# Beginning the expert weights' transfers from two engines instead of one, in a two-block transformer kernel on one Trainium2 core

## The chip, the cores and the metric

One core of one Trainium2 chip. The metric is the device time of one launch in microseconds (us), the median of the runs shown. The kernel is one program with five instruction streams: TensorE (PE), VectorE (DVE), ScalarE (ACT), GpSimd (POOL) and SyncE (SP). The streams meet only at semaphores. A transfer (DMA) is begun by one of the streams and then moved by 16 DMA engines, which all streams share.

## What is computed

Two transformer blocks run one behind the other on 256 tokens of width 1024, all in float32. The first block has two mixers and a gated convolutional feed-forward part. The second has a pooling mixer, latent attention, and then the part that this change touches, a mixture of 32 experts of which each token uses 4:

```python
logits = ht @ w_router + b_router
top_vals, top_idx = top_k(logits, 4); gates = softmax(top_vals)
...
gu   = xblk @ w_gate_up[e] + b_gate_up[e]        # 1024 -> 2048
gate = minimum(gu[:, :1024], 7); up = clip(gu[:, 1024:], -7, 7)
act  = gate * sigmoid(1.702 * gate) * (up + 1)
yb   = act @ w_down[e] + b_down[e]               # 1024 -> 1024
y[token] += gate_of_token * yb
```

Every expert brings 8 MB of `w_gate_up` and 4 MB of `w_down`, whatever number of tokens it has. The 32 experts together are 12.58 MB x 32 = 402.7 MB.

## The kernel before

**Jobs.** A job is 64 token slots of one expert. An expert with more than 64 tokens has a second job, which uses the same weights again. PE runs the jobs in one loop (`job_turn`, L2246). A job is, in order: the gate and up product in four pairs of weight chunks (`gate_up`, L2112, its matmuls at L2127), with the combining matmuls of the job before after the second and third pair (L2162); the turn of the gate weights, the gathering of the next job's tokens, the turn of the activations and the next job's bias (L2149 to L2151, L2108, L2140, L1950); and the down product in two halves (`down`, L2190, its matmuls at L2203).

**Buffers.** An expert's weights stand in twelve slots, which are taken two by two as six places of 2 MB: pairs 0 to 3 for gate and up, and down halves 0 and 1. Three more places (`stage`, AHEAD = 3) hold pairs 0 to 2 of the expert behind it. So pairs 0 to 2 are loaded into `stage` and copied by GpSimd into their places (L599, four copies for a pair), while pair 3 and the down halves are loaded straight into theirs. A place is free when PE has used it: `gu_used` counts pairs 0 to 2, `gu_full` counts pair 3, `d_used` the quarters of the down product. For an expert with two jobs it is the second job that frees them (`last_job`, read from a table). For the last six experts (from STAGED = 26 on) there is no staging; pairs 0 to 2 too are loaded straight into their places when these are free.

**Who begins what.** Before the change SP begins every one of these transfers, 192 of 2 MB, in one order written out by hand, and it waits at each in turn. For one expert m of the main loop (L428 to L435):

```python
next_last_pair(m, last)      # wait gu_full of expert m,  begin pair 3 of m + 1
next_stage(m, 0)             # wait pair 0 of m + 1 copied, begin pair 0 of m + 2
for h in range(2):
    next_down(m, last, h)    # wait d_used of m, begin down half h of m + 1
next_stage(m, 1)
next_stage(m, 2)
```

In the six experts without staging (L440 to L447) the order is pairs 0, 1, 2, 3 and the halves 0, 1. In the table of issues, L373 is a pair into its place, L376 a pair into `stage`, L379 a down half and L444 a pair of the unstaged experts.

**GpSimd's stream** (`gpsimd_program`, L462) does small work for the first block and attention, among it two subtractions for the output projection (L585, PE reads their results at L2041), the reciprocal roots (`rsqrt`, L483), and then the loop of copies (L591 to L600): for each of the pairs 0 to 2 it waits until the staged pair has landed and until PE has used that pair's place, and copies.

**The start.** Expert 0's six places and expert 1's staged pairs are loaded during attention, as buffers come free; `jobs_ready` (the order of the jobs) then opens the loops. The places lie partly over the attention's buffers, so each of these loads has a wait of its own (L382 to L399).

Of the kernel before, what the change touches and what calls it, by code (L numbers as in the profile page):

```python
# [32 lines left out]
P = 128  # L33
# [237 lines left out]

def slot_use(n):

    return n % RING, 16 * (n // RING + 1)
# [32 lines left out]
def sync_program(g, sp):  # L307
# [61 lines left out]
    gate_up = w["w_gate_up_2"].rearrange("e (c p i) n -> e c p (i n)", p=P, i=2)  # L369
    down = w["w_down_2"].rearrange("e (h p i) n -> e h p (i n)", h=2, p=P)  # L370
# [6 lines left out]

    def load_down(e, h):
        sp.dma_start(pair_slot(g, PAIRS + h), down[e, h]).then_inc(s.job_landed(GU + 2 * h), 16)  # L379
# [8 lines left out]
    load_gu(0, 3)  # L388
    load_down(0, 1)
# [7 lines left out]
    load_down(0, 0)  # L397
# [12 lines left out]
    def next_last_pair(m, last):  # L410

        sp.wait_ge(s.gu_full, last * 2 + 2)
        load_gu(m + 1, PAIRS - 1)

    def next_down(m, last, h):

        sp.wait_ge(s.d_used, last * DN + (2 * h + 2))
        load_down(m + 1, h)

    sp.wait_ge(s.jobs_ready, 1)  # L420
    last = last_job(0)
    next_stage(0, 0)
    next_stage(0, 1)
    next_last_pair(0, last)
    next_stage(0, 2)
    for h in range(2):
        next_down(0, last, h)
    with sp.Fori(1, STAGED - 2) as m:  # L428
        last = last_job(m)
        next_last_pair(m, last)  # L430
        next_stage(m, 0)
        for h in range(2):
            next_down(m, last, h)
        next_stage(m, 1)
        next_stage(m, 2)  # L435
    last = last_job(STAGED - 2)
    next_last_pair(STAGED - 2, last)
    for h in range(2):
        next_down(STAGED - 2, last, h)
    with sp.Fori(STAGED - 1, E - 1) as m:  # L440
# [4 lines left out]
        next_last_pair(m, last)  # L445
        for h in range(2):
            next_down(m, last, h)  # L447
# [14 lines left out]
def gpsimd_program(g, pool):  # L462
# [117 lines left out]
    pool.tensor_tensor(t.diff[:], t.diff[:], t.u_pad[:, :, 16:], ALU.subtract).then_inc(s.diff_ready, 1)  # L580
    rsqrt("pool")
    for c in range(2):
# [5 lines left out]
    rsqrt("moe")  # L588

    pool.wait_ge(s.jobs_ready, 1)  # L590
    with pool.Fori(0, STAGED - 1) as m:  # L591
        last = pool.value_load(t.job_last[0:1, bass.ds(m, 1)], min_val=0, max_val=E + OVER - 1)
        for pair in range(AHEAD):
# [6 lines left out]
            ins.then_inc(s.in_place[pair], 16)  # L600

# [978 lines left out]
def tensor_program(g, pe):  # L1580
# [531 lines left out]
    def gate_up(m, o, e, pair):  # L2112
# [3 lines left out]
        if m is None or pair == PAIRS - 1:  # L2116
            pe.wait_ge(*expert_landed(g, e, 2 * pair))
        else:
            pe.wait_ge(s.in_place[pair], e * 16 + 16)
# [70 lines left out]
    def down(m, o, e):  # L2190
# [454 lines left out]
```

## Time and profile before

| what | value |
|---|---|
| time, median of 3 runs | 1493.42 us (1492.33 to 1495.0) |
| the profiled execution: span from first to last instruction | 1490.6 us |
| median less the profiled span | 2.8 us |
| mean granted TensorE clock | 0.989 of full speed |
| bytes read from HBM | 479.26 MB, 322 GB/s over the span |
| first transfer of an expert's weights begun | 484.17 us |
| order of the jobs known, loop of copies starts | 548.19 us |
| last byte of the weights lands | shortly after 1470 us |

No time beside its span is given for the profiled execution itself, so its own time is taken as the span and the 2.8 us that the median has over it; the lowest run is 1.7 us over the span.

How to read it: the page gives the busy time of each engine and cuts the span into 40 slices of 37.3 us, with the busy tenths of each engine and of the DMA engines and the GB/s moved. The chain of waits follows the work that ended last back to what released it. A timeline lists an engine's instructions in order of time, with the idle time before one and what ended it. The windows give the busy time of each engine and the DMA share in chosen stretches.

### The profile page before, as it was taken

To read this page: it belongs to the slowest core of one execution; us is meant where nothing else is said; L and a number is where in the kernel's file an instruction comes from. 1 tells how busy PE (TensorE), PEld (TensorE's weight loads), DVE (VectorE), ACT (ScalarE), POOL (GpSimd) and SP (SyncE) were. 2 spreads that over 40 slices of the span, in tenths; PEclk is the share of its full clock that TensorE was granted. 3 is DMA by queue.
4 is the path that set the end of the run, shared out by engine and by line. 5 is a ranking of instruction groups with operands and counts; after the bars stand their busy time and mean duration, and the time that the engine had idled before them with its cause. 6 is when DMAs were issued, how large, how long until landed. Compare 5 with 4: busy or idle time off the path is not lost.

```text
span 1490.6 us, 20373 instructions
## 1 busy us (share of the span) xinstructions
PE 1415.9 (95%) x7344; PEld 781.2 (52%) x7345; DVE 650.3 (44%) x1102; ACT 248.9 (17%) x424; POOL 416.3 (28%) x432
## 2 busy tenths in 40 slices
PE   8999999999989999999999999999999999999995
PEld 7668867999976664343333343343333334333332
DVE  3134735677654553344443344444444434333333
ACT  1222113444423420010001010010000001000001
POOL 3000011222216233334433435444443444200000
PEclk9999999999999999999999999999999999999998
DMA  8433344455533878999996999999999999999995
GB/s 276 147 136 113 113 134 149 170 196 174 177 126 135 300 283 358 429 427 427 429 427 276 429 429 427 427 427 428 429 427 427 427 428 429 427 427 429 427 429 226
DMA packets 77413, 480.73 MB, mean 323 GB/s; under 512 B 7019, under 2 KB 31272, under 8 KB 52808
## 3 DMA queue, kind: packets, MB, share of 16 engines
q1 hardware_dynamic: 74046, 477.45, 78.6%
q10 hardware_dynamic: 3338, 2.88, 0.6%
q8 instruction: 20, 0.33, 0.1%
q14 instruction: 9, 0.07, 0.0%
HBM read 479.26 MB, written 1.05 MB: 322 GB/s over the span
## 4 chain that ended last, share of the span: by engine, by line
PE 51%; DMA 39%; POOL 5%; DVE 3%; issue 1%; ACT 1%; SPq 0%; POOLq 0%; ACTq 0%; DVEq 0%
DMA stage<-in_w_gate_up 28%; PE bank L2127 10%; PE bank L1866 8%; PE bank L1614 8%; DMA ring<-in_w_gate_up 7%; PE bank L1624 6%; PE bank L2203 5%; POOL ring L599 5%; PE bank L1878 4%; PE bank L1798 2%; DMA ring_b<-in_w_gate_up 2%; DMA ring_b<-in_w_down 2%; PE bank L2108 1%; PE bank L1675 1%; PE bank L2162 1%
## 5 line engine op out<-in xcount | busy, mean ns | idle before, releaser
L599 POOL COPY ring<-stage 128x1024 f32<-128x1024 f32 x300 | 310.3, 1080 | 443.7 <-DMA stage<-in_w_gate_up 359.7
L2127 PE MATMUL bank<-ring,x_T 128*64 128x512 f32 x1584 | 368.0, 610 | 38.1 <-POOL ring L599 31.3
L2127 PEld LDWEIGHTS bank<-ring,x_T 128*64 128x64 f32 x1584 | 111.0, 140 | 272.6 <-issue 205.9
L2203 PE MATMUL bank<-ring_b,act_T 128*64 128x512 f32 x1056 | 236.1, 596 | 1.1 <-ACT act_T L872 0.5
L1494 DVE TENSOR_TENSOR h<-h,bank 128x512 f32<-128x512 f32 x128 | 82.2, 683 | 243.9 <-PE bank L2162 243.9
L2203 PEld LDWEIGHTS bank<-ring_b,act_T 128*64 128x64 f32 x1056 | 72.0, 137 | 147.9 <-issue 125.7
L2127 PE MATMUL bank<-ring_b,x_T 128*64 128x512 f32 x528 | 120.6, 598 | 2.3 <-DMA ring_b<-in_w_gate_up 2.3
L1470 DVE SCALAR_TENSOR_TENSOR y_lo<-bank,slot_gate,y_hi 128x512 fp32r<-128x512 f32 x33 | 24.8, 751 | 194.8 <-ACT y_hi L852 194.8
L866 ACT ACTIVATE sig<-bias_raw 128x512 f32<-128x512 f32 x33 | 20.8, 629 | 509.5 <-DVE bias_raw L1500 509.5
L1866 PE MATMUL bank<-h_hi,ff_hi 128*128 128x256 f32 x352 | 99.8, 284 | 1.9 <-POOL h_lo L531 1.4
L1866 PE MATMUL bank<-h_lo,ff_hi 128*128 128x256 f32 x352 | 99.6, 283 | 0.0
L1866 PE MATMUL bank<-h_hi,ff_lo 128*128 128x256 f32 x352 | 99.6, 283 | 0.0
L1614 PE MATMUL bank<-x_nT,ring 128*128 128x256 f32 x448 | 98.1, 380 | 0.0
L524 POOL TENSOR_TENSOR ff_lo<-ring,ff_hi 128x2048 fp32r<-128x2048 f32 x11 | 51.0, 4640 | 159.0 <-PE bank L1866 111.1
L1614 PEld LDWEIGHTS bank<-x_nT,ring 128*128 128x128 f32 x448 | 84.7, 190 | 12.2 <-issue 0.8
L2127 PEld LDWEIGHTS bank<-ring_b,x_T 128*64 128x64 f32 x528 | 35.0, 136 | 71.3 <-issue 67.2
L1866 PEld LDWEIGHTS bank<-h_hi,ff_hi 128*128 128x128 f32 x352 | 67.5, 192 | 2.8 <-issue 1.7
L2108 PE MATMUL bank<-picks,h_half 128*128 128x128 f32 x512 | 68.1, 286 | 0.0
L738 ACT ACTIVATE ff_hi<-ring 128x2048 fp32r<-128x2048 f32 x33 | 61.8, 1903 | 35.6 <-DMA ring<-in_w_ffn_in 35.6
L1866 PEld LDWEIGHTS bank<-h_lo,ff_hi 128*128 128x128 f32 x352 | 67.5, 192 | 0.4
L1866 PEld LDWEIGHTS bank<-h_hi,ff_lo 128*128 128x128 f32 x352 | 67.5, 192 | 0.0
L2108 PEld LDWEIGHTS bank<-picks,h_half 128*128 128x128 f32 x512 | 62.8, 196 | 0.8 <-issue 0.8
(435 smaller groups left out, 1609.4 us busy)
## 6 DMA issues: line engine op xcount, KB each, us to landing
stage<-in_w_gate_up SPq DMA_DIRECT2D x75, 2048.0 KB, 25.0
ring_b<-in_w_down SPq DMA_DIRECT2D x64, 2048.0 KB, 23.0
ring_b<-in_w_gate_up SPq DMA_DIRECT2D x32, 2048.0 KB, 20.9
ring<-in_w_gate_up SPq DMA_DIRECT2D x21, 2048.0 KB, 25.5
ring<-in_w_in SPq DMA_DIRECT2D x22, 1024.0 KB, 7.2
ring<-in_w_ffn_in SPq DMA_DIRECT2D x22, 1024.0 KB, 5.1
ring<-in_w_ffn_out SPq DMA_DIRECT2D x11, 1024.0 KB, 4.7
ring<-in_w_out SPq DMA_DIRECT2D x8, 1024.0 KB, 6.1
```

The source lines that it names most:

```text
L524: pool.tensor_tensor(t.ff_lo[:, 1, :], t.ring[:, slot, :], t.ff_hi[:, slot, :].bitcast(F32), ALU.subtract).then_inc(s.ff_lo_pool, 1)
L599: ins = pool.tensor_copy(pair_slot(g, pair)[:, cols], t.stage[:, pair, cols])
L738: act.activation(t.ff_hi[:, n % RING, :], t.ring[:, n % RING, :], ACT.Copy).then_inc(s.ff_hi_done, 1)
L1494: dve.tensor_tensor(t.h[:, b, cols], t.h[:, b, cols], g.banks[2 + c][:], ALU.add).then_inc(s.added, 1)
L1614: ins = pe.matmul(bank[:, j * T:(j + 1) * T], wk[:, f * P:(f + 1) * P], src[:, k, :], start=(k == 0), stop=(k == len(weights) - 1))
L1624: ins = pe.matmul(bank[:, 0:n], src[:, k, b * P:(b + 1) * P], wk[:, c0:c0 + n], start=(k == 0), stop=(k == len(weights) - 1))
L1798: ins = pe.matmul(bank[:, q * T:(q + 1) * T], chunk(g, n, (4, 512))[:, k, P * (f % 4):P * (f % 4) + P], (t.o_sb, t.o_glaT)[q][:, k, :], st ...
L1866: ins = pe.matmul(bank[:, f * T:(f + 1) * T], wt[:, k, f * P:(f + 1) * P], ht[:, k, :], start=(k == 0 and part == 0), stop=(k == KT - 1 an ...
L1878: ins = pe.matmul(banks[2 * b + c][:], ut[:, q, k, b * P:(b + 1) * P], wt[:, k, 512 * c:512 * c + 512], start=False, stop=last, skip_group ...
L2108: ins = pe.matmul(banks[6][:, f * P:(f + 1) * P], t.h_half[:, b, k_rows], t.picks[:, b, :], start=(b == 0), stop=(b == 1))
L2127: ins = pe.matmul(banks[n][rows, :], t.x_T[:, c, :], job_slot(g, c)[:, c0:c0 + 512], start=False, stop=(c == GU - 1), skip_group_check=True)
L2203: ins = pe.matmul(banks[4][rows, :], t.act_T[:, k, SLOTS * (c // 2):SLOTS * (c // 2) + SLOTS], job_slot(g, GU + c)[:, c0:c0 + 512], start= ...
```

## The change

SP keeps only what it loads into `stage` (and pairs 0 to 2 of the unstaged experts). GpSimd begins pair 3 and both down halves of every expert, behind its copies for the same expert. Pair 3 and the halves count on semaphores of their own.

```diff
@@ SP, start
     sp.dma_start(t.b_down[0:E, :], w["b_down_2"]).then_inc(s.b_down_in, 16)
-    load_gu(0, 3)
-    load_down(0, 1)
...
     load_gu(0, 2)
-    load_down(0, 0)
     for pair in range(1, AHEAD):
         load_stage(1, pair)
@@ SP, loops
+    for pair in range(AHEAD):
+        next_stage(0, pair)
+    with sp.Fori(1, STAGED - 2) as m:
+        for pair in range(AHEAD):
+            next_stage(m, pair)
     sp.wait_ge(s.jobs_ready, 1)
-    last = last_job(0)
-    next_stage(0, 0)
-    next_stage(0, 1)
-    next_last_pair(0, last)
-    next_stage(0, 2)
-    for h in range(2):
-        next_down(0, last, h)
-    with sp.Fori(1, STAGED - 2) as m:
-        last = last_job(m)
-        next_last_pair(m, last)
-        next_stage(m, 0)
-        for h in range(2):
-            next_down(m, last, h)
-        next_stage(m, 1)
-        next_stage(m, 2)
-    last = last_job(STAGED - 2)
-    next_last_pair(STAGED - 2, last)
-    for h in range(2):
-        next_down(STAGED - 2, last, h)
     with sp.Fori(STAGED - 1, E - 1) as m:
         last = last_job(m)
         for pair in range(AHEAD):
             sp.wait_ge(s.gu_used, last * AHEAD + (pair + 1))
             sp.dma_start(pair_slot(g, pair), gate_up[m + 1, pair]).then_inc(s.in_place[pair], 16)
-        next_last_pair(m, last)
-        for h in range(2):
-            next_down(m, last, h)
@@ GpSimd
+    def load_last_pair(e):
+        pool.dma_start(pair_slot(g, PAIRS - 1), gate_up[e, PAIRS - 1]).then_inc(s.pair_landed, 16)
+    def load_down(e, h):
+        pool.dma_start(pair_slot(g, PAIRS + h), down[e, h]).then_inc(s.half_landed[h], 16)
+    def next_straight(m, last):
+        pool.wait_ge(s.gu_full, last * 2 + 2)
+        load_last_pair(m + 1)
+        for h in range(2):
+            pool.wait_ge(s.d_used, last * DN + (2 * h + 2))
+            load_down(m + 1, h)
+
     rsqrt("pool")
+    pool.wait_ge(*g.r2.drained("s7"))
+    load_last_pair(0)
+    load_down(0, 1)
     for c in range(2):
...
     rsqrt("mla")
     rsqrt("moe")
+    pool.wait_ge(*g.r2.filled("pa11"))
+    load_down(0, 0)
 
     pool.wait_ge(s.jobs_ready, 1)
     with pool.Fori(0, STAGED - 1) as m:
...
             ins.then_inc(s.in_place[pair], 16)
+        next_straight(m, last)
+    with pool.Fori(STAGED - 1, E - 1) as m:
+        next_straight(m, last_job(m))
@@ PE
-        if m is None or pair == PAIRS - 1:
+        if pair == PAIRS - 1:
+            pe.wait_ge(s.pair_landed, e * 16 + 16)
+        elif m is None:
             pe.wait_ge(*expert_landed(g, e, 2 * pair))
...
-                pe.wait_ge(*expert_landed(g, e, GU + c))
+                pe.wait_ge(s.half_landed[c // 2], e * 16 + 16)
```

## Rows read from the trace of the kernel before

**Rows 1.** The page: busy tenths and GB/s of the DMA engines in 40 slices.

```profile
DMA  8433344455533878999996999999999999999995
GB/s 276 147 136 113 113 134 149 170 196 174 177 126 135 300 283 358 429 427 427 429 427 276 429 429 427 427 427 428 429 427 427 427 428 429 427 427 429 427 429 226
```

**Rows 2.** Chain of waits, a combining, and one steady turn: start us, us, what.

```profile
828.68 0.67 PE bank L2162 x4
...
985.83 25.03 DMA stage<-in_w_gate_up
1011.09 4.00 POOL ring L599 x4
```

**Rows 3.** Windows over the steady stretch; columns PE, PEld, DVE, ACT, POOL, PEclk, DMA share, GB/s.

```profile
1000.00:1100.00 100.00, 93.53 (x465) 36.63 (x465) 40.44 (x70) 8.61 (x21) 39.93 (x38) 0.98 1.01 428
```

**Rows 4.** Timeline of PE, job start without a stall (650 us) and with stalls (1009 us).

```profile
624.50 7.04 PE L2127 MATMUL bank<-ring,x_T 128*64 128x512 f32 x32
...
650.71 7.04 PE L2127 MATMUL bank<-ring,x_T 128*64 128x512 f32 x32
...
1009.48 3.60 PE L2127 MATMUL bank<-ring,x_T 128*64 128x512 f32 x16
1015.13 3.65 PE L2127 MATMUL bank<-ring,x_T 128*64 128x512 f32 x16 [2.05 <-POOL ring L599]
```

**Rows 5.** Timeline of SP's queue, steady stretch: the fourth pair and a staged pair.

```profile
998.74 0.34 SPq L373 DMA_DIRECT2D ring_b<-in_w_gate_up  x1
1001.55 0.33 SPq L376 DMA_DIRECT2D stage<-in_w_gate_up  x1
```

**Rows 6.** Timeline of GpSimd, the steady stretch: the copy of pair 0.

```profile
996.39 4.98 POOL L599 COPY ring<-stage 128x1024 f32<-128x1024 f32 x4 [5.82 <-DMA stage<-in_w_gate_up]
```

**Rows 7.** Windows at the loops' start and the first DMA gap, columns as in rows 3.

```profile
552.00:556.00 4.00, 3.93 (x21) 1.32 (x19) 3.79 (x6) 0.45 (x2) 4.00 (x5) 1.00 0.73 213
...
584.00:588.00 4.00, 4.00 (x23) 1.48 (x21) 2.57 (x4) 0.63 (x1) 3.74 (x4) 1.00 0.17 74
588.00:592.00 4.00, 4.00 (x31) 3.23 (x33) 1.73 (x4) 1.10 (x4) 0.00 (x0) 1.00 0.81 262
```

**Rows 8.** Timelines there: GpSimd's copies of three pairs, then SP's next issues.

```profile
575.87 11.88 POOL L599 COPY ring<-stage 128x1024 f32<-128x1024 f32 x12 [15.27 <-PE bank L2127]
...
587.82 0.35 SPq L373 DMA_DIRECT2D ring_b<-in_w_gate_up  x1
588.45 0.34 SPq L376 DMA_DIRECT2D stage<-in_w_gate_up  x1
```

**Rows 9.** Windows at the second gap, columns as in rows 3.

```profile
792.00:796.00 4.00, 4.00 (x22) 1.38 (x20) 2.09 (x9) 0.10 (x1) 1.03 (x2) 1.00 0.88 373
...
804.00:808.00 4.00, 4.00 (x26) 2.05 (x23) 2.60 (x4) 1.07 (x3) 2.85 (x3) 1.00 0.09 20
```

**Rows 10.** Timelines there: the second job of expert 8 (PE), copies, SP's issue behind it.

```profile
791.19 7.04 PE L2127 MATMUL bank<-ring,x_T 128*64 128x512 f32 x32
...
794.97 11.87 POOL L599 COPY ring<-stage 128x1024 f32<-128x1024 f32 x12 [22.70 <-PE bank L2127]
...
806.93 0.34 SPq L373 DMA_DIRECT2D ring_b<-in_w_gate_up  x1
```

**Rows 11.** The end: PE's last fourth pair and last down product, and the DMA window.

```profile
1462.77 3.65 PE L2127 MATMUL bank<-ring_b,x_T 128*64 128x512 f32 x16 [0.58 <-DMA ring_b<-in_w_gate_up]
...
1469.64 7.09 PE L2203 MATMUL bank<-ring_b,act_T 128*64 128x512 f32 x32 [0.47 <-ACT act_T L872]
...
1468.00:1472.00 4.00, 3.11 (x16) 1.47 (x18) 0.36 (x1) 0.66 (x2) 0.00 (x0) 1.00 0.65 274
```

**Rows 12.** Attention: GpSimd's two subtractions and PE's first use of their results.

```profile
499.08 9.02 POOL L585 TENSOR_TENSOR ring_r<-ring,pa_hi 128x2048 fp32r<-128x2048 f32 x2 [4.62 <-ACT pa_hi L827]
...
515.84 0.40 PE L2041 MATMUL bank<-ring_r,ya_hi 128*128 128x512 f32 x1
```

**Rows 13.** Window in which only transfers with 2 KB rows (w_in) are in flight.

```profile
20.00:25.00 5.00, 5.00 (x25) 4.41 (x24) 0.00 (x0) 1.11 (x2) 0.00 (x0) 1.00 1.11 357
```

More of the change, by code:

```diff
@@ L269, in _, with expert_weights @@
             tensor_program(g, pe)
+def expert_weights(w):
+    return (w["w_gate_up_2"].rearrange("e (c p i) n -> e c p (i n)", p=P, i=2),
+            w["w_down_2"].rearrange("e (h p i) n -> e h p (i n)", h=2, p=P))
 def slot_use(n):
@@ L365, in sync_program @@
         load(g.n_second + n, src, shape)
-    gate_up = w["w_gate_up_2"].rearrange("e (c p i) n -> e c p (i n)", p=P, i=2)
-    down = w["w_down_2"].rearrange("e (h p i) n -> e h p (i n)", h=2, p=P)
+    gate_up, _ = expert_weights(w)
     def load_gu(e, pair):
@@ L376, in load_stage @@
         sp.dma_start(t.stage[:, pair, :], gate_up[e, pair]).then_inc(s.staged[pair], 16)
-    def load_down(e, h):
-        sp.dma_start(pair_slot(g, PAIRS + h), down[e, h]).then_inc(s.job_landed(GU + 2 * h), 16)
     sp.wait_ge(*g.r2.filled("pm1"))
@@ L408, in next_stage @@
         load_stage(m + 2, pair)
[L410 to L418, printed above, removed]
-    sp.wait_ge(s.jobs_ready, 1)
-    last = last_job(0)
-    next_stage(0, 0)
-    next_stage(0, 1)
-    next_last_pair(0, last)
-    next_stage(0, 2)
-    for h in range(2):
-        next_down(0, last, h)
-    with sp.Fori(1, STAGED - 2) as m:
-        last = last_job(m)
-        next_last_pair(m, last)
-        next_stage(m, 0)
-        for h in range(2):
-            next_down(m, last, h)
-        next_stage(m, 1)
-        next_stage(m, 2)
-    last = last_job(STAGED - 2)
-    next_last_pair(STAGED - 2, last)
-    for h in range(2):
-        next_down(STAGED - 2, last, h)
+    for pair in range(AHEAD):
[3 more added lines that the diff above has]
+            next_stage(m, pair)
+    sp.wait_ge(s.jobs_ready, 1)
     with sp.Fori(STAGED - 1, E - 1) as m:
@@ L580, in gpsimd_program, with last_job @@
     pool.tensor_tensor(t.diff[:], t.diff[:], t.u_pad[:, :, 16:], ALU.subtract).then_inc(s.diff_ready, 1)
+    gate_up, down = expert_weights(g.w)
+    def load_last_pair(e):
+        pool.dma_start(pair_slot(g, PAIRS - 1), gate_up[e, PAIRS - 1]).then_inc(s.pair_landed, 16)
+    def load_down(e, h):
+        pool.dma_start(pair_slot(g, PAIRS + h), down[e, h]).then_inc(s.half_landed[h], 16)
+    def last_job(e):
+        return pool.value_load(t.job_last[0:1, bass.ds(e, 1)], min_val=0, max_val=E + OVER - 1)
+    def next_straight(m, last):
[4 more added lines that the diff above has]
+            load_down(m + 1, h)
     rsqrt("pool")
+    pool.wait_ge(*g.r2.drained("s7"))
+    load_last_pair(0)
+    load_down(0, 1)
     for c in range(2):
@@ L588, in gpsimd_program @@
     rsqrt("moe")
+    pool.wait_ge(*g.r2.filled("pa11"))
+    load_down(0, 0)
     pool.wait_ge(s.jobs_ready, 1)
     with pool.Fori(0, STAGED - 1) as m:
-        last = pool.value_load(t.job_last[0:1, bass.ds(m, 1)], min_val=0, max_val=E + OVER - 1)
+        last = last_job(m)
         for pair in range(AHEAD):
@@ L2399, in __init__ @@
         self.place_free = new("place_free")
+        self.pair_landed = new("pair_landed")
+        self.half_landed = [new(f"half_landed{h}") for h in range(2)]
         self.in_place = [new(f"in_place{n}") for n in range(AHEAD)]
```

## The prediction

> **What bounds the kernel now.** I read the slices first: from the seventeenth on the DMA engines are busy nine tenths or more and move 427 to 429 GB/s, except in the slice at 783 us (276 GB/s) and in the last [rows 1]. The window over 100 us of that stretch says the same: DMA share 1.01, 428 GB/s [rows 3]. So from about 590 us the kernel is bound by bytes. One expert is 12.58 MB, at 428 GB/s 29.4 us, or 4.9 us for each of its six transfers. The chain of waits shows how this looks from inside: a staged transfer takes 25.03 us, its copy 4.00 us, and with some 0.2 us between them the turn is 29.4 us [rows 2]. The 25 us are no latency to be saved; they are five transfers of 4.9 us that stand ahead in the one queue. PE alone needs less: a job without a stall starts 26.21 us after the one before it (624.50 to 650.71) [rows 4]. So PE is idle 3.2 us per expert, and the DMA engines are not.
>
> Two gaps in the DMA's work are all that an order of issue can win. The first is at 584 to 592 us (shares 0.17 and 0.81, so 3.3 + 0.8 = 4.1 us idle) [rows 7]. GpSimd has copied three pairs by 587.75, the first of them by 579.9, but SP stands at the fourth pair's wait until 587.82 and begins the staged pair behind it at 588.45 [rows 8]. The second is the only place where an expert has two jobs. The DMA engines run dry at about 795.5 us (share 0.88 of a window of 4 us) and are idle until about 807.6 (0.09) [rows 9]. The second job starts at 791.19, the copies at 794.97, the first copy is done at 799.0, and SP again comes to it only behind the fourth pair at 806.93 [rows 10].
>
> **The change part by part.**
>
> *SP loses 96 of its 192 issues and all waits for PE in the staged stretch.* SP's own time is no bound (0.33 us an issue) [rows 5]. What goes is the block: a staged pair is begun as soon as it is copied. At the first gap that is 579.9 instead of 588.45, so the DMA engines stay busy: 4.1 us won. At the second it is 799.0 instead of 806.93: 7.9 us won, if PE stands where it stood.
>
> *GpSimd gets 96 issues.* No row shows an issue by GpSimd. The nearest are SP's 0.33 us [rows 5] and, on GpSimd itself, one copy, 4.98/4 = 1.2 us at its longest [rows 6]; I take 1.2 us. Three of them are 3.7 us per expert, beside 12 to 13 us of copies in a period of 29.4 us: hidden by GpSimd's idle time (5.82 us ahead of that copy alone). If this cover were gone, the copy of pair 0 would be late, and it has slack: it ends at 1001.4, PE needs it at 1009.48 [rows 4, 6]. In attention two issues come ahead of the subtractions, into the 4.62 us in which GpSimd idles, and their results are first read at 515.84, 7.7 us after they end [rows 12]. At nothing, then; if an issue cost 4 us or more, PE would begin to wait there.
>
> The copy of 4.98 us, where the undisturbed one takes 4.00 [rows 2, 6], shows that GpSimd can be held up by about 1 us in a pair. The Trainium skill (SBUF — State Buffer, Who interferes with whom) says that VectorE in a two-port mode locks GpSimd out, and that a transfer begun by GpSimd then waits for its descriptors. It speaks against this change; by it a begin would be late by the length of a VectorE instruction, which the sum doesn't need while the other queue has work.
>
> *Order behind the copies.* GpSimd begins pair 3 of expert m+1 behind the copy of its pair 2, where SP needed only `gu_full` of m. Behind the waiting GpSimd stand both down halves and the next copies. In before's steady stretch pair 3 is begun at 998.74 [rows 5], while the copy of pair 1 starts only at 1011.09 [rows 2]: the old order of landings would not survive. What settles in its place I work out next.
>
> *Two queues instead of one.* This is the term that decides. In one queue the bytes arrive in the order in which PE uses them. In two, with three transfers of an expert each, I assume equal shares: each then gets 9.8 us per transfer while both have work. Bounds: GpSimd's queue served first is nearly the old order; SP's served first ends as below, since SP can be ahead by its three staged places only. When the down half 1 of expert e lands, SP's queue has then moved as many transfers as GpSimd's: all of the staged pairs of e+1 and 0.9 of the first of e+2. Before, it was only the first of e+1. So 2.9 transfers, 14 us of bytes, come ahead of what PE waits for. PE waits for down halves instead of staged pairs, and stands later behind the same bytes. The rate itself stays: with both queues never empty the period is still 29.4 us.
>
> Put into numbers at the second gap: GpSimd's 21 transfers for experts 1 to 7 and SP's 21.9 are 42.9 x 4.902 = 210.3 us. From the loops' first byte at 553.1 (share 0.73 of the window from 552) [rows 7] that is 763.4, and 1.8 us between last byte and landing (worked out at the end, below) make 765.2. Half a down product later (7.09/2 = 3.55) [rows 11] expert 8 starts, at 768.8, and its second job 26.2 later at 795.0, 3.8 after the 791.19 of before. The DMA engines drain early, but they restart by PE: before, the first copy was done 7.8 us after the job's start (799.0), so now at 802.8, against SP's 806.93. **Won: 4.1 us**; of the 4.1 and 7.9 together, two thirds are given back. Behind it the bytes run without a gap, as before.
>
> *The end.* Before, the last byte arrives at about 1470.6 (share 0.65 of a 4 us window); the wait for the fourth pair ended at 1462.77, and the down product ends at 1476.73 [rows 11], 13.96 us later. In the new order the last SP transfer (pair 2 of expert 31) lands while GpSimd's queue still has 1.3 to 1.55 transfers, 6.3 to 7.6 us; I take 7.0. With a last byte at 1470.6 - 4.1 = 1466.5 that is 1459.5, and 1.8 us from byte to landing (before: 1470.6 - 9.8 = 1460.8, landed 1462.6) make 1461.3. PE then does pair 2 (3.6) [rows 4] and a combining (0.67) [rows 2] ahead of the same tail: 1461.3 + 0.15 + 3.6 + 0.67 = 1465.7, + 13.96 = 1479.7 against 1476.73. **Lost: 7.1 us at the end, 3.0 net of the 4.1 won.**
>
> The 1.3 to 1.55 are found so: PE has used pair 2 of expert 30 at a time S, which begins pair 2 of 31; SP's queue, always full, lands it 29.4 - 3.6 = 25.8 later. Down half 1 of expert 30 lands 9.0 to 11.6 after S (pair 3, turns, gathering and a half product lie between), and in the 14.2 to 16.8 us that are left GpSimd's queue moves 1.45 to 1.7 of its last three.
>
> Sum: 1490.6 + 3.0 = 1493.6 us of span; with the 2.8 us that the median has over the span, 1496.4, which is 3.0 over the median 1493.42.
>
> **The rivals.** A measurement of this kernel can tell about 0.2% (3 us) from no change; that bounds "same".
>
> *A, forecast: bytes bound, PE pushed back by the equal shares.* 1493.5 to 1502: the loss of 7.1 may be 4 to 10 and the 4.1 won 1.5 to 4.1 (issues of 1.2 us and small gaps make PE later still). For it: the full DMA share. Against: the equal share is an assumption. Chance 0.42, a third of it under 1496.4.
>
> *B, faster: GpSimd's queue is served promptly, PE keeps its place.* Then both gaps close: 4.1 + 7.9 = 12.0 us, 1481.4; with half of that, 1487. Decided by whether the down halves land as early against the staged pairs as before. For it: the gaps are real and SP's block is what holds them. It takes an uneven share, or GpSimd's queue being mostly the shorter. Chance 0.22.
>
> *C, no change: the gain at the second gap is larger or the last pair less late, and they cancel.* 1490.4 to 1496.4; 1493.4 if 3 us of the tail's loss fall away. Chance 0.18.
>
> *D, clearly slower: transfers begun by GpSimd move less per us.* Nothing in the trace has one. If they moved as those with 2 KB rows did, 357 instead of 428 GB/s [rows 13], half the 402.7 MB would take 564 instead of 470 us: +94. The other way no slice moves over 429 [rows 1], which is 2 us less for all of it. I take none, since both queues move the same 16 KB rows; 2% on that half is +9, 5% is +24. It decides from about 1% on. Chance 0.18, mostly 1502 to 1525.
>
> The Trainium skill (DMA: Bandwidth & Descriptors, Queues, rings and completion order) has each DMA engine take turns between queues packet by packet; with rows of equal length that gives the equal shares of A. The same page (Issuing engines are not separate DMA queues) says that beginning on several engines saves only issue time, by which nothing but C is left.
>
> Range: A and C whole, of B the nearer half, of D the nearer part: 1485 to 1512. The likeliest case alone: 1493.5 to 1502. Faster by over 0.2%: B and a little of C, 0.25. Within: the rest of C and a third of A, 0.29. Slower: two thirds of A, and D, 0.46.
>
> **What would show it.** In the chain of waits the staged transfer should give way to down halves, pair 3 and unstaged pairs; PE should wait 2 to 3 us per expert at the down product (L2203); staged pairs should land well before their copy. The share at 584 to 592 should be 1.0; the second gap should start earlier than 795.5 and end near 803. DMA share and 428 GB/s elsewhere should stay, and PE's last fourth pair should start later relative to the last byte. Wrong would be: a rate below 420 or above 432 GB/s, gaps in each period (GpSimd's order starves the DMA), or a second job that starts no later than 791.

## The result and the profile after

| | kernel before | changed kernel |
|---|---|---|
| median | 1495.76 us (1492.33 to 1498.94, 6 runs) | 1505.65 us (1501.65 to 1507.97, 6 runs) |
| ratio, 95% interval | | 1.0065 [1.0047, 1.0083] |

The change makes the kernel slower by 0.65%. The forecast had the side (slower) and the range (1485 to 1512), but not the size: +3.0 us against +9.9 (a second comparison, below, gives +9.9 again). The measured time lies above the likeliest case alone (1493.5 to 1502); only the width that was added for rival D reaches it. The profiled execution spans 1505.2 us.

In the changed kernel the gate and up product stands at L2131, the down product at L2207, GpSimd's copies at L598, its begins of pair 3 at L557 and of the down halves at L561, and SP's staged pairs at L381. The page of the changed kernel (slices, queues, chain, groups with busy time, mean ns and idle time before, issues with us to landing):

```profile
DMA  8433343555525679999995999999999999999993
GB/s 274 157 123 112 112 160 125 189 176 188 184 91 178 252 301 427 428 428 426 429 428 215 430 427 428 428 426 429 427 428 428 426 429 428 392 429 428 429 427 132
...
q1 hardware_dynamic: 60222, 276.11, 46.4%
q0 software_dynamic: 13824, 201.33, 31.5%
...
DMA ring_b<-in_w_down 31%; PE bank L2207 10%; PE bank L2131 10%; PE bank L1868 8%; PE bank L1616 7%; DMA ring<-in_w_gate_up 7%; PE bank L1626 6%; PE bank L1880 4%; PE bank L1800 2%; PE bank L2110 1%; PE bank L1677 1%; PE bank L2166 1%; PE bank L2025 1%; PE bank L1952 0%; PE bank L2097 0%
...
L2207 PE MATMUL bank<-ring_b,act_T 128*64 128x512 f32 x1056 | 249.0, 620 | 40.6 <-DMA ring_b<-in_w_down 40.1
...
L561 POOL DMA_DIRECT2D ring_b<-in_w_down x64 | 33.9, 529 | 297.8 <-PE bank L2207 297.8
...
stage<-in_w_gate_up SPq DMA_DIRECT2D x75, 2048.0 KB, 21.0
ring_b<-in_w_down POOLq DMA_DIRECT2D x64, 2048.0 KB, 21.6
ring_b<-in_w_gate_up POOLq DMA_DIRECT2D x32, 2048.0 KB, 15.6
```

The rate is what it was, 426 to 430 GB/s [rows 1]. The slice of the second gap (at 783 us before, at 790 us now) has gone from 276 to 215 GB/s, and there is a new dip, 392 GB/s, in the slice that begins at 1279 us, where staging ends. PE now waits at the down product for down halves: 40.1 us over the loops. The chain confirms the turn foretold: 25 us of a down half, then half a down product, where a staged transfer and its copy stood [rows 2]. That half product takes 3.7 us, or 5.4 us where the granted clock fell from 2.4 to 1.2 GHz behind the wait (0.57 of full speed in the window 1084:1088; PE had been busy 1.35 of the 4 us before). The chain around 1060 us:

```profile
1058.51 25.05 DMA ring_b<-in_w_down
1083.56 0.04 issue
1083.61 5.38 PE bank L2207 x16
```

The DMA view of the same kernel's window 1000:1100 (queue: packets, MB, share of 16 engines) and its line in the windows answer to [rows 3]:

```profile
q1 hardware_dynamic: 1469, 21.45, 50.5%
q0 software_dynamic: 1461, 21.32, 50.1%
```

```profile
1000.00:1100.00 100.00, 93.25 (x458) 35.62 (x454) 32.17 (x74) 7.95 (x19) 51.07 (x54) 0.98 1.01 428
```

Here the two queues, which both have work, share the engines equally, to 1%, at the old rate of 428 GB/s. So rival D (GpSimd's transfers are slower) is out, and A's assumption of equal shares holds.

The first gap is closed: the windows 584:588 and 588:592 have shares of 1.02 and 1.00, where there were 0.17 and 0.81 [rows 7]. The second gap in the changed kernel, in windows:

```profile
792.00:796.00 4.00, 4.00 (x29) 3.01 (x31) 1.61 (x3) 1.10 (x4) 0.00 (x0) 1.00 0.29 123
...
808.00:812.00 4.00, 4.00 (x22) 1.31 (x20) 1.28 (x2) 0.00 (x0) 4.00 (x5) 1.00 0.35 70
...
1280.00:1284.00 4.00, 3.92 (x28) 2.83 (x28) 2.38 (x5) 1.06 (x4) 4.00 (x4) 1.00 0.61 258
1284.00:1288.00 4.00, 4.00 (x20) 1.29 (x18) 1.07 (x3) 0.00 (x0) 0.65 (x2) 1.00 0.77 246
```

These places have to be counted from the start of the loops: GpSimd's began 3.6 us later in this execution, at 551.8 instead of 548.19 us. Ahead of that PE's granted clock was 0.83 of full speed in 508:512, 0.50 (1.2 GHz) in 512:520 and 0.89 in 520:524, after PE had been busy 3.03 of the 4 us in 504:508; the repeat below, with 3.15 there, had 1.00 throughout, and its loops began at 547.86. The account is made on the repeat.

### The profile page after: what moved, and what is told of

Read it like the earlier page. It is cut to its first block, busy times and chain, and to the rows that moved or that the text cites. A ratio compares the mean times of both kernels' runs of the same rounds, so it can differ in the third digit from the quotient of the medians.

```text
span 1505.2 us, 20326 instructions
## 1 busy us (share of the span) xinstructions
PE 1422.4 (94%) x7344; PEld 788.3 (52%) x7345; DVE 601.2 (40%) x1102; ACT 248.9 (17%) x424; POOL 473.0 (31%) x528
## 4 chain that ended last, share of the span: by engine, by line
PE 56%; DMA 37%; DVE 3%; issue 1%; ACT 1%; POOL 0%; POOLq 0%; SPq 0%; DVEq 0%; ACTq 0%
DMA ring_b<-in_w_down 31%; PE bank L2207 10%; PE bank L2131 10%; PE bank L1868 8%; PE bank L1616 7%; DMA ring<-in_w_gate_up 7%; PE bank L1626 6%; PE bank L1880 4%; PE bank L1800 2%; PE bank L2110 1%; PE bank L1677 1%; PE bank L2166 1%; PE bank L2025 1%; PE bank L1952 0%; PE bank L2097 0%
## 5 line engine op out<-in xcount | busy, mean ns | idle before, releaser
L598 POOL COPY ring<-stage 128x1024 f32<-128x1024 f32 x300 | 316.1, 1106 | 157.8 <-PE bank L2131 84.6
L2131 PE MATMUL bank<-ring,x_T 128*64 128x512 f32 x1584 | 356.7, 599 | 8.0 <-DMA ring<-in_w_gate_up 7.6
L2207 PE MATMUL bank<-ring_b,act_T 128*64 128x512 f32 x1056 | 249.0, 620 | 40.6 <-DMA ring_b<-in_w_down 40.1
L2131 PEld LDWEIGHTS bank<-ring,x_T 128*64 128x64 f32 x1584 | 111.1, 138 | 229.8 <-issue 219.6
L2207 PEld LDWEIGHTS bank<-ring_b,act_T 128*64 128x64 f32 x1056 | 73.7, 142 | 198.6 <-issue 128.6
L561 POOL DMA_DIRECT2D ring_b<-in_w_down x64 | 33.9, 529 | 297.8 <-PE bank L2207 297.8
L2131 PE MATMUL bank<-ring_b,x_T 128*64 128x512 f32 x528 | 120.6, 598 | 0.0
L2131 PEld LDWEIGHTS bank<-ring_b,x_T 128*64 128x64 f32 x528 | 35.0, 136 | 68.7 <-issue 68.6
L854 ACT ACTIVATE y_hi<-bank,slot_gate 128x512 fp32r<-128x512 f32 x33 | 22.7, 687 | 287.1 <-PE bank L2207 287.1
```

The source lines that it names most:

```text
L561: pool.dma_start(pair_slot(g, PAIRS + h), down[e, h]).then_inc(s.half_landed[h], 16)
L598: ins = pool.tensor_copy(pair_slot(g, pair)[:, cols], t.stage[:, pair, cols])
L2131: ins = pe.matmul(banks[n][rows, :], t.x_T[:, c, :], job_slot(g, c)[:, c0:c0 + 512], start=False, stop=(c == GU - 1), skip_group_check=True)
L2207: ins = pe.matmul(banks[4][rows, :], t.act_T[:, k, SLOTS * (c // 2):SLOTS * (c // 2) + SLOTS], job_slot(g, GU + c)[:, c0:c0 + 512], start= ...
```

## The experiments

Each was timed beside the kernel before (medians of before 1493.05, 1493.0 and 1493.51 us in the three groups, 20 to 23 runs each). In the order in which they ran.

### 1. The changed kernel again

> The changed kernel once more, unaltered, as the yardstick for the runs beside it. Theory 1 (equal shares of two queues put staged pairs ahead of what PE waits for, so PE is pushed back; GpSimd's transfers themselves are as fast): about 1505 us, gap at the expert with two jobs from 793 to 810 us, last staged landing well ahead. In its first profile the loops of experts started 3.6 us later than before (551.8 against 548.2 us), beside a granted TensorE clock of half speed from 512 to 520 us. If the change causes that, the loops start near 551.8 again and the clock falls at the same place; if it is chance, it may start near 548 and the run is about 4 us shorter.

Measured: 1502.94 us (1501.32 to 1506.71), ratio 1.0072 [1.0055, 1.0089]; profiled span 1499.7 us. The timelines around expert 8's second job (PE, GpSimd, SP), two windows, PE's end, and SP's last store:

```profile
796.25 7.04 PE L2131 MATMUL bank<-ring,x_T 128*64 128x512 f32 x32
...
800.04 11.85 POOL L598 COPY ring<-stage 128x1024 f32<-128x1024 f32 x12 [28.65 <-PE bank L2131]
...
804.21 8.17 SPq L381 DMA_DIRECT2D stage<-in_w_gate_up  x3
```

```profile
788.00:792.00 4.00, 4.00 (x25) 1.80 (x25) 1.65 (x4) 0.66 (x2) 0.00 (x0) 1.00 0.27 115
...
804.00:808.00 4.00, 4.00 (x20) 1.24 (x20) 1.28 (x2) 0.00 (x0) 4.00 (x6) 1.00 0.72 217
...
1276.00:1280.00 4.00, 4.00 (x21) 1.45 (x22) 1.69 (x4) 0.66 (x2) 2.13 (x3) 1.00 0.45 131
...
1468.00:1472.00 4.00, 4.00 (x20) 1.21 (x18) 1.89 (x3) 0.00 (x0) 0.00 (x0) 1.00 0.67 279
```

```profile
1465.17 3.65 PE L2131 MATMUL bank<-ring,x_T 128*64 128x512 f32 x16 [1.23 <-DMA ring<-in_w_gate_up]
1469.41 3.65 PE L2131 MATMUL bank<-ring_b,x_T 128*64 128x512 f32 x16
...
1476.28 7.09 PE L2207 MATMUL bank<-ring_b,act_T 128*64 128x512 f32 x32 [0.47 <-ACT act_T L874]
...
1492.88 0.35 SPq L422 DMA_DIRECT2D out<-h  x1
```

The second job starts at 796.25 instead of 791.19 (+5.1); the first staged pair behind it is begun at 804.21, where SP's first begin was at 806.93 [rows 10]. The last byte comes at 1468 + 0.67 x 4 = 1470.7, as before (1470.6), but the down product ends at 1483.37, 12.7 us behind it, where it was 6.1 [rows 11].

This execution (1501.32 us) is the fastest of its six, and in it PE stands earlier than in the others. Counted from the start of the loops, in us (a version is the experiment of that number, here and below):

| profiled execution | second job of expert 8 | SP's first begin behind the gap | last byte | down product's end behind it | program's end behind that |
|---|---|---|---|---|---|
| before | 243.0 | 258.7 | 922.4 | 6.1 | 13.9 |
| version 2 (below) | 248.2 | 256.1 | 919.6 | 6.6 | 13.8 |
| version 1 | 248.4 | 256.3 | 922.8 | 12.7 | 16.3 |
| changed kernel, first profile | 250.3 | 258.2 | 925.0 | 12.1 | 16.3 |
| version 5 | 250.8 | 258.8 | 925.2 | 13.2 | 16.3 |
| version 7, first | 251.6 | 259.6 | 926.4 | 13.1 | 16.3 |
| version 8 | 250.2 | 258.2 | 925.1 | 7.8 | 14.0 |

So the restart behind the gap, 2.4 us earlier than before in version 1, is between 0.6 us earlier and 0.9 us later in the four other executions with two queues, and the last byte is 2.6 to 4.0 us later instead of 0.4. What decides between the two is not shown. The two columns at the end hardly move between executions of one kind.

### 2. The order alone, with one queue

```diff
@@ before, SP
     with sp.Fori(1, STAGED - 2) as m:
         last = last_job(m)
+        for pair in range(AHEAD):
+            next_stage(m, pair)
         next_last_pair(m, last)
-        next_stage(m, 0)
         for h in range(2):
             next_down(m, last, h)
-        next_stage(m, 1)
-        next_stage(m, 2)
```

(and likewise for expert 0, ahead of the loop).

> The kernel before with one queue only, SP beginning all, but in the order that the changed kernel has: staged pairs 0, 1, 2 of expert m+2, then pair 3 and the down halves of m+1. Theory 1: the bytes that come ahead of a down half are two transfers more than before (9.8 us), where two queues make it 2.9 to 3.4. Against the kernel before the second job starts about 3 us later (794), the DMA engines restart 4 to 5 us earlier (802 to 803), the first gap is closed and the end of the kernel is as before, since the unstaged experts keep their order: 1490 to 1494 us where before has 1495.8. Theory 2 (transfers begun by GpSimd are slow): there are none here, so at or below the kernel before. Theory 3 (pair 3 and the halves begun behind the copies starve the DMA or PE): as slow as the changed kernel, 1502 to 1506, with gaps in each period.

Measured: 1490.81 us (1488.03 to 1492.79), ratio 0.9986 [0.9977, 0.9996]; profiled span 1488.0. Its second job starts at 796.19 us, its first staged pair is begun at 804.15: both within 0.1 us of version 1's. So the order alone pushes PE by 5.2 us, with no second queue. But it does so by another wait. PE's waits for transfers between 600 and 790 us (in all, times, longest), in version 1 and in this version:

```profile
PE bank L2207 <- DMA ring_b<-in_w_down: 9.5, 5, 2.8
```

```profile
PE bank L2126 <- DMA ring_b<-in_w_gate_up: 10.0, 5, 3.1
```

Here PE waits for pair 3, ahead of which all three staged pairs now stand; in version 1 it waits for down halves. The agreement to 0.1 us is at least in part chance: in four of the five traces of two queues in the table the push is 7.2 to 8.6 us. In this version the push costs nothing: the last six experts are in the old order, PE has caught up by the end (down product ends at 1474.18), and the last byte comes at about 1467.6, 3.0 us earlier than before. Of the changed kernel's +9.9 us, then, the order of the staged stretch is -2.2, and the rest, +12.1, is what the second queue adds. By the two profiled executions (1499.7 less 1488.0 = 11.7) these are 3.1 of a later last byte, 6.1 of a later end behind it (12.7 against 6.6) and 2.5 behind the down product (16.3 against 13.8).

### 3. One staged pair ahead of pair 3, with one queue

```diff
@@ before, SP
     with sp.Fori(1, STAGED - 2) as m:
         last = last_job(m)
-        next_last_pair(m, last)
         next_stage(m, 0)
+        next_last_pair(m, last)
```

> The kernel before with one line moved: SP begins the staged pair 0 of expert m+2 ahead of pair 3 of m+1 (no other order changed, one queue). Theory 1: the first gap closes (4.1 us), at the second gap one transfer of 4.9 us fits into the 7.9 us, PE's lag hardly grows: 1487 to 1491 us where before has 1495.8. Theory 3: pair 3 is begun 2.8 us later in each steady period, PE waits for it and the gain is lost: 1494 to 1498.

Measured: 1488.72 us (1487.01 to 1490.73), ratio 0.9972 [0.9959, 0.9985]: faster than both kernels. The first gap is closed here too (window 584:588 at 1.07), and the second job is not pushed: it starts at 786.87. SP begins staged pair 0 at 794.82, as soon as it is copied. This is much of the gain that the change was after, for one line moved.

### 4. Pair 3 begun by GpSimd ahead of its copy of pair 2

```diff
@@ changed, GpSimd, loop of copies
         for pair in range(AHEAD):
             pool.wait_ge(s.staged[pair], m * 16 + 16)
             pool.wait_ge(s.gu_used, last * AHEAD + (pair + 1))
+            if pair == AHEAD - 1:
+                next_last_pair(m, last)
...
-        next_straight(m, last)
+        next_halves(m, last)
```

> The changed kernel with GpSimd beginning pair 3 of expert m+1 ahead of its copy of pair 2 instead of behind it. Theory 1: no change against the changed kernel (within 2 us, about 1505), since its queue is never empty when pair 3 is begun. Theory 3: half or more of the 10 us come back, 1495 to 1500. Theory 2: no change.

Measured: 1574.35 us (1573.09 to 1575.99), ratio 1.0545 [1.0528, 1.0563], which no theory had. VectorE's group in the window 1000:1100, the window, and PE's and GpSimd's timelines:

```profile
L1517 DVE SCALAR_TENSOR_TENSOR act<-bias_raw 128x512 f32<-128x512 f32 x4 | 18.0, 4497 | 0.1
```

```profile
1000.00:1100.00 100.00, 87.91 (x414) 34.89 (x416) 42.65 (x68) 7.92 (x20) 42.60 (x48) 0.93 0.98 407
```

```profile
998.24 4.50 DVE L1517 SCALAR_TENSOR_TENSOR act<-bias_raw 128x512 f32<-128x512 f32 x1
...
998.21 3.98 POOL L603 COPY ring<-stage 128x1024 f32<-128x1024 f32 x4
...
1002.79 0.75 PE L2151 MATMUL bank<-ident,act 128*128 128x128 f32 x4 [3.10 <-DVE act L1517]
```

The copy of pair 2 now begins when PE has finished the gate and up product (gu_full), at the moment at which VectorE works on the SwiGLU. Its last operation, both of whose inputs lie in SBUF, takes 4.50 us instead of 0.69, as long as the copy; PE waits 3.10 us for it in each job of this stretch, and the rate falls to 407 GB/s.

### 5. The same, with the copy kept off VectorE's operation

```diff
@@ version 4, GpSimd, behind next_last_pair
+                pool.wait_ge(s.act_ready, last + 1)
```

> The version that took 1574 us (the changed kernel with pair 3 begun ahead of the copy of pair 2), and in it GpSimd now waits, ahead of the copy of pair 2, until VectorE's SwiGLU for that job is done. Theory G (the 79 us came from GpSimd's copy running beside VectorE's operation with two inputs in SBUF, which then took 4.5 us instead of 0.7 and kept PE waiting 3.1 us per job): that operation is back at 0.7 to 0.8 us, PE no longer waits 3 us for act, period 29.4 us, and the time falls to 1497 to 1506 us. Rival (the time came from pair 3 standing ahead in GpSimd's queue, that is from the order of the bytes): it stays above 1550. Between: 1510 to 1530 if the later copy of pair 2 itself becomes the new wait.

Measured: 1504.65 us (1502.69 to 1511.41), ratio 1.0088 [1.0066, 1.0111]. The group is back, and so is the rate (428 GB/s):

```profile
L1518 DVE SCALAR_TENSOR_TENSOR act<-bias_raw 128x512 f32<-128x512 f32 x4 | 2.8, 692 | 0.1
```

One wait gives back 70 us, with pair 3 still early in the queue: the collision was the cause. And pair 3 early or late in GpSimd's queue makes no difference that was measured (1504.65 against 1502.94, ranges overlapping).

### 6. One GpSimd transfer, and 32

The kernel before, with the load of the down biases moved to GpSimd, as one transfer:

```diff
-    sp.dma_start(t.b_down[0:E, :], w["b_down_2"]).then_inc(s.b_down_in, 16)
...
+    pool.wait_ge(*g.r2.drained("s7"))
+    pool.dma_start(t.b_down[0:E, :], g.w["b_down_2"]).then_inc(s.b_down_in, 16)
```

> The kernel before, with one single transfer changed hands: GpSimd instead of SP begins the load of the down biases (128 KB, at the start). Disputed: the 2.4 us by which the changed kernel's program goes on longer behind its last down product (16.3 us against 13.9 us) although its output stores begin and move alike. Theory F (a fixed cost at program end as soon as GpSimd has a queue of its own): the span behind the last down product grows from 13.9 to about 16.3 us, and the median by 2 to 3 us over the kernel before, ratio 1.0015 to 1.002. Rival (it comes from many transfers outstanding on that queue, or from a PE clock or a landing by chance): 13.9 us as before, ratio 1.000.

Measured: 1493.89 us, ratio 1.0009 [0.9999, 1.0018]; the profiled execution ends 4.4 us after SP's last store is begun (1486.64, span 1491.0), as before (1486.21, 1490.6). The fixed cost is not there. With 32 transfers of one row:

```diff
+    for e in range(E):
+        pool.dma_start(t.b_down[e:e + 1, :], g.w["b_down_2"][e:e + 1, :]).then_inc(s.b_down_in, 16)
```

> The kernel before, and the down biases (128 KB) are loaded by GpSimd in 32 transfers of one row instead of one of SP. One GpSimd transfer had left the program's end at 4.4 us behind VectorE's last instruction; the changed kernel with 96 has 6.85 us. Theory N (the end grows with the number of transfers that GpSimd has begun): 5.2 us with 32 of them, +0.8. Rival P (it grows with the packets or bytes of that queue, or with transfers begun inside a loop): 4.4 us, unchanged. Their issues take some 17 us of GpSimd at 470 to 490 us; if that delays the subtractions for the output projection, the start moves by up to 5 us, which is read off separately.

Measured: 1492.76 us, ratio 0.9993 [0.9983, 1.0003], and again 4.4 us (1492.34, 1496.7). The number of begins is not it either.

### 7. Staging kept up to the last experts

`STAGED = E - 2` instead of `E - 6` in the changed kernel:

> The changed kernel with staging kept up for experts up to 30 (STAGED = E - 2) instead of 26. The changed kernel shows a DMA gap of 2.3 to 3.2 us where staging ends, because SP's queue has run dry there while GpSimd's has only its share; before has none. Theory T (the gap comes from SP waiting for PE to free a place of the first unstaged expert, which it now reaches early): the gap moves from 1280 us to about 1400 us and stays about as long, and the last pairs stay late, so that the time is within 2 us of the changed kernel's, 1502 to 1506. Rival (the six unstaged experts are what makes the tail late, since SP there is no longer ahead): the wait for the last SP transfer moves by several us; the time falls by 3 to 7 us, to 1496 to 1500.

Measured: 1505.72 us (1502.37 to 1508.02), ratio 1.0083 [1.007, 1.0096]. The dip has moved along, to the window 1396:1400 (share 0.46, so 2.2 us), as foretold. PE no longer waits for any SP transfer at the end, yet its down product still ends 13.1 us behind the last byte (1487.7 against 1474.6):

```profile
1453.73 7.09 PE L2207 MATMUL bank<-ring_b,act_T 128*64 128x512 f32 x32
...
1480.60 7.09 PE L2207 MATMUL bank<-ring_b,act_T 128*64 128x512 f32 x32 [0.47 <-ACT act_T L874]
```

PE's last wait for any transfer ends at 1375.22, for a down half of expert 27. From there it works without waiting for a transfer and still comes 13 us behind the last byte. So the end is set here by PE's own late place, with no late transfer; in version 1 the wait for the last SP transfer (1.23 us) comes on top.

`STAGED = E - 1` in version 3 (one queue):

> One queue, staged pair 0 begun ahead of pair 3 (the version at 1488.7 us, under both kernels), with staging kept up for all experts but the last (STAGED = E - 1). Theory: the end is set by the last bytes and what PE must still do behind them; with one queue there is no gap where staging ends, so it is within 1.5 us of 1488.7. Rival: staging the last experts too lets their pairs 0 to 2 land earlier than PE frees their places, the DMA engines are kept fuller at the end, and 2 to 5 us are won: 1484 to 1487.

Measured: 1489.67 us, ratio 0.998 [0.9971, 0.9989]: as the theory had it, no gain.

### 8. The last six experts with one queue

```diff
@@ changed, GpSimd
     with pool.Fori(STAGED - 1, E - 1) as m:
-        next_straight(m, last_job(m))
+        last = last_job(m)
+        for pair in range(AHEAD):
+            pool.wait_ge(s.gu_used, last * AHEAD + (pair + 1))
+            pool.dma_start(pair_slot(g, pair), gate_up[m + 1, pair]).then_inc(s.tail_in[pair], 16)
+        next_straight(m, last)
@@ changed, SP, in place of its loop over the unstaged experts
+    with sp.Fori(1, E - STAGED + 1) as m:
+        for pair in range(AHEAD):
+            sp.wait_ge(s.tail_in[pair], m * 16)
+            sp.sem_inc(s.in_place[pair], 16)
```

> The changed kernel, and in the last six experts (those without staging) GpSimd begins all six transfers in the order of the kernel before, pairs 0, 1, 2, 3 and the halves; SP begins none there and only passes their landing on. So one queue instead of two from 1280 us on, everything ahead of it as changed. Theory (the loss at the end is the equal share of two queues, by which the last SP transfer lands 5.5 us before the last byte and not 9.8): the wait for the last pair 2 at L2131 goes away, the last wait is again that for pair 3, the down product ends 13 to 14 us behind it as before, and 5 to 7 us are won: 1496 to 1498 us. The 2.4 us at the very end stay. Rival (PE is late at the end because of its pushed place, whatever the queues): 1501 to 1504, as the changed kernel.

Measured: 1497.89 us (1493.81 to 1501.07), ratio 1.0024 [1.0012, 1.0035]; profiled span 1496.4. PE's end and SP's last store:

```profile
1466.79 3.65 PE L2134 MATMUL bank<-ring_b,x_T 128*64 128x512 f32 x16 [0.54 <-DMA ring_b<-in_w_gate_up]
...
1491.94 0.35 SPq L421 DMA_DIRECT2D out<-h  x1
```

The last wait is again that for pair 3, 7.9 us before the last byte (1466.79 and 1474.7; in before 1462.77 and 1470.6, so 7.8). Over its own before it stands at +4.4 us where version 1 stands at +9.9: 5.5 us won, as the theory had it. A surprise: the 2.4 us at the program's end are gone as well (1491.94 to 1496.4 is 4.5 us; in version 1, 1492.88 to 1499.7 is 6.8), though GpSimd begins more transfers than ever. The two gains read in the trace, 4.9 us (12.7 less 7.8) and 2.4, are more than the 5.5 of the medians, since its last byte comes 2.3 us later after the loops' start than version 1's. That is not of the edit's doing: its second job of expert 8, ahead of all that was edited, already started 3.6 us later than version 1's (799.82), half of it because its loops began at 549.62. Its last down product also took 8.78 us instead of 7.09, at a granted clock between 1.2 and 2.4 GHz (0.78 in 1472:1476; PE had been busy 3.15 of the 4 us before). Counted from the start of the loops, its span is 5.0 us shorter than version 1's, near the 5.5 of the medians. The dip at 1280 us (share 0.40) stays.

### 9. SP held back in the staged stretch

```diff
@@ changed, SP
     with sp.Fori(1, STAGED - 2) as m:
-        for pair in range(AHEAD):
-            next_stage(m, pair)
+        last = last_job(m)
+        next_stage(m, 0)
+        sp.wait_ge(s.d_used, last * DN + 4)
+        next_stage(m, 1)
+        next_stage(m, 2)
```

> The changed kernel, but SP is held back in the staged stretch: it begins pair 0 of expert m + 2 as soon as it may, and pairs 1 and 2 only once PE has used the down halves of m, about where the kernel before had them. Two queues still, the tail as changed. Theory (what pushes PE's second job of expert 8 from 791 to 796 us is that all three staged pairs are ahead of the down halves, not that there are two queues): the second job starts at 788 to 792, PE no longer waits 2.7 us per expert at the down product, the DMA engines restart at 799 to 800 us, and 3 to 5 us are won: 1498 to 1500 us. Rival (two queues push PE whatever SP does): second job at 795 or later, 1502 to 1505. It could also lose in each period, if the held pairs land late for their copies: then DMA gaps in each period and over 1510.

Measured: 1544.17 us (1543.61 to 1551.28), ratio 1.0338 [1.0324, 1.0352]: the outcome that stood there as a warning. GpSimd's timeline:

```profile
1003.16 4.92 POOL L602 COPY ring<-stage 128x1024 f32<-128x1024 f32 x4 [6.69 <-DMA stage<-in_w_gate_up]
1012.97 4.00 POOL L602 COPY ring<-stage 128x1024 f32<-128x1024 f32 x4 [4.89 <-DMA stage<-in_w_gate_up]
1016.91 0.53 POOL L561 DMA_DIRECT2D ring_b<-in_w_gate_up  x1
```

GpSimd waits 6.69 and 4.89 us for staged pairs, and only behind the copy of the last of them begins pair 3, at 1016.91. The DMA engines have run low by then (rate 414 GB/s in 1000:1100, against 428), PE waits up to 4.7 us for a down half, and a turn takes 30.9 us on average instead of 29.4 (GpSimd begins pair 3 at 1016.91 and, eight turns on, at 1264.18). So with pair 3 behind the copies, SP has to run ahead in this kernel: the order that pushes PE is also what keeps this kernel's DMA engines fed. The question the run was made for, whether two queues push PE when SP does not run ahead, it does not answer; only version 2 speaks to it.

Both edits (8 and 9) together:

> The last two edits together on the changed kernel: SP held back in the staged stretch, and one queue (GpSimd's) in the last six experts. Theory (the three losses, pushed PE, the end, and the 2.4 us behind the last store, are separate): the gains add up, 1492 to 1495 us, about the kernel before, with both DMA gaps shortened and 2.4 us at the program's end left over. Rival: they overlap, 1496 or more.

Measured: 1537.34 us, ratio 1.0289 [1.0269, 1.0309]. They add up (1544.17 less 5.5 would be 1538.7), but on the side of the loss.

## Why the prediction was right in its side and wrong in its size

The account, profiled executions of version 1 less before, in us; they began their loops 0.3 us apart, and version 1 is the favourable one of the table above:

| step | predicted | measured | from |
|---|---|---|---|
| DMA engines restart behind the second gap | -4.1 | -2.7 | 804.21 against 806.93 |
| gap where staging ends | 0 | +2.2 | (1 - 0.45) x 4 |
| rest of the bytes, not accounted for | 0 | +0.6 | remainder |
| last byte (the three rows above) | -4.1 | +0.1 | 1470.7 against 1470.6 |
| down product's end behind the last byte | +7.1 | +6.6 | 12.7 against 6.1 |
| program's end behind that | 0 | +2.5 | 16.3 against 13.9 |
| sum of the last three (rounded parts) | +3.0 | +9.1 | 1499.7 against 1490.6 |

**Bytes bound, equal shares, rate kept:** right, with 50.5% and 50.1%, 428 GB/s. The turn is bound by bytes as before, and PE waits for down halves.

**GpSimd's begins at 1.2 us, hidden:** right that they are hidden; one takes 0.53 us, under half of what was taken.

**PE pushed back, second gap:** the step was right in kind and too small in size. The last down half of expert 7 was worked out to land at 765.2, 217.0 us after the loops' start. In version 1 PE goes on from there at 218.7:

```profile
766.55 3.65 PE L2207 MATMUL bank<-ring_b,act_T 128*64 128x512 f32 x16 [1.30 <-DMA ring_b<-in_w_down]
```

In the four other executions with two queues it goes on at 220.4 to 221.1, and in one of them (version 7) the half product behind it then takes 5.23 us instead of 3.65. So the second job, put at 795.0, came at 796.25, and the restart won 2.7 us and not 4.1; in the other four, counted from the loops' start, it won at most 0.6, where the forecast's lower bound was 1.5. The reason given was too narrow, too: the order alone, in one queue, pushes PE by 5.2 us (version 2).

**The end:** +7.1 forecast, +6.6 found. The forecast hung it on the landing of the last SP transfer, 5.2 us ahead of the last byte; PE went on 5.5 us ahead of it. But version 7 shows that PE's late place alone gives the same 13 us, so the good number is in part luck. Version 8, which undoes both by returning to one queue, has the old 7.9 us from the last wait to the last byte again.

**What failed** is the 4.1 us won at the second gap (the term just named), the line "Behind it the bytes run without a gap, as before", and that nothing was looked for behind the last down product. (1) Where staging ends, SP's next begin needs PE to have used a place of expert 25; in before its queue still held pair 3 and down halves then, but now those are GpSimd's. SP begins nothing from 1248.7 to 1287.3, GpSimd nothing from 1258.7 until pair 3, behind its copies, at 1277.60, and both queues run dry for 2.2 us. The dip's move with STAGED (version 7) shows that it belongs to this place; the copy ahead of pair 3 is not what makes it, for with pair 3 ahead of the copy (version 5) 1.8 us of it remain (shares 0.93 and 0.62 in 1280:1288). (2) The program ends 2.4 to 2.5 us later behind its last stores. One GpSimd transfer or 32 do not cause it, nor does a queue of 114 (version 8). It is in all six traces in which SP begins unstaged pairs beside GpSimd's straight ones (the changed kernel, versions 1, 4, 5, the first of 7, the first of 9), and in none of the eight others. Its cause stays open. In version 1 these two and the 1.4 us at the second gap are 2.2 + 2.5 + 1.4 = 6.1, the whole distance between the forecast (+3.0) and the account (+9.1); the remainder of +0.6 and the end's 0.5 less than forecast nearly cancel.

**What was luck.** The measured time is in the range only by the part that was added for D, transfers of GpSimd that move less per us, and the runs show no such thing. By its own mechanism the forecast ended at 1502, 8.6 us over the median before; it came out at 9.9.

**The rivals.** B (both gaps closed, PE in place) is what version 3 does with one queue: 4.3 us under before, less than B's 12, since its second gap is only broken up (share 0.15 in 792:796, then 0.90, 0.61, 0.84). C and D are out: the time is slower clear of the noise, and the rate is the old one. The Trainium skill (DMA: Bandwidth & Descriptors, Issuing engines are not separate DMA queues) has several issuing engines save issue time only; the runs disagree in effect: the queues interleave, as the page says, but by interleaving they change the order of landings, and one queue instead of two in the last six experts gave 5.5 us back. The prediction took from the Trainium skill (SBUF — State Buffer, Who interferes with whom) only that VectorE can hold GpSimd up. The same section has a VectorE instruction with two SBUF inputs contend with a GpSimd instruction that reads SBUF, and says that the issue order decides who blocks. In version 4 the trace agrees: GpSimd's copies began 0.03 us ahead and ran undisturbed (3.98 us), and VectorE's operation waited until all four were done.

## What to carry to other kernels

When transfers leave one in-order queue for two, ask first in what order the bytes will then land, not how fast they are begun: here two busy queues got half each, and the one with the more urgent bytes lost. Look at the places where one queue's supply changes (a phase that ends, the last items), for there the shares turned into a gap and a late tail; and try the reordering within the one queue first, which here gave a gain (1488.72 us, 4.3 us under before) without the price. And profile one kernel more than once before an account of single microseconds is made on it: here the restart behind the gap moved by 3.3 us between executions that are alike up to there. Before a GpSimd copy is moved, look at what VectorE does at that moment.

## What the hardware showed unexpectedly

- A GpSimd copy and a VectorE operation with both inputs in SBUF that begin together did not run side by side: 0.69 us became 4.50 us (version 4), over the four copies of a pair back to back (3.98 us), and 70 us of kernel time hung on it. In the changed kernel itself the copy of pair 2 meets the operation before that one (L1504), whose mean over the kernel is 1.03 us (0.87 in before), and the copy then takes 4.9 us.
- A transfer of 2 MB is begun by GpSimd in 0.53 us, by SP in 0.33 us [rows 5]; GpSimd's queue alone moves 429 GB/s (version 8, window 1300:1400), both together 428.
- 2.4 to 2.5 us at the program's end go with SP and GpSimd both beginning weights in the last stretch. The last stores are begun and land alike (3.8 to 3.9 us from begin to landing in before and in version 1), and nothing in the trace stands beside the difference.
- In version 1 the half product behind a wait of 2.79 us for a down half took 5.35 us instead of 3.65 (at 678.29 and 737.12): in 678:682 the granted clock was 0.64 of full speed, partly 1.2 GHz instead of 2.4, where PE had been busy 1.49 of the 4 us before. Behind waits of 1.3 us it took 3.65. The length of the wait alone doesn't decide it: in before, behind 2.05 us, it was 5.35 us once (at 1044.56) and 3.65 another time (at 1015.13).
